# Packing three column groups into one expert unit of a mixture-of-experts layer: 46 units in place of 52

## What is computed

```python
gates = jnp.einsum('tk,tke->te', wsel, jax.nn.one_hot(eidx, N_EXPERTS, dtype=wsel.dtype))
def expert(acc, xs):
    wg, wu, wd, ge = xs
    y = (jax.nn.silu(x @ wg) * (x @ wu)) @ wd
    return acc + ge[:, None] * y.astype(jnp.float32), None
routed, _ = lax.scan(expert, jnp.zeros((n_tok, shp[-1]), jnp.float32), (w_gate, w_up, w_down, gates.T))
```

## Time and profile before

| | us |
|---|---|
| median of 3 runs | 1839.17 |
| lowest and highest | 1833.34, 1845.14 |
| the profiled execution | 1832.0 |
| its span, first to last instruction | 1830.3 |

### The profile page before, as it was taken

The page is one execution under the profiler, slowest core; times in us unless marked ns, Lnnn a source line. Parts: engine busy times, 40 slices in busy tenths (PEclk is TensorE's granted clock), DMA queues, the critical chain, the costliest instruction groups (busy, mean ns, idle before and its releaser), DMA issues. The chain is left out here.

```text
span 1830.3 us, 19726 instructions
## 1 busy us (share of the span) xinstructions
PE 1645.5 (90%) x7369; PEld 952.7 (52%) x7369; DVE 669.5 (37%) x1267; ACT 340.6 (19%) x680; POOL 323.3 (18%) x338
## 2 busy tenths in 40 slices
PE   5998888999858979999687987999999999999966
PEld 3856665664347767877473443344444444444423
DVE  2001333343378493442454973241111111111128
ACT  1001233423222121222110220011111111111120
POOL 5000000000039990000000251011111111111100
PEclk8996899999988999999798999999999999999989
DMA  9213010113131214230924004999999999989756
GB/s 342 81 46 101 24 47 1 47 47 109 56 96 52 99 62 116 83 114 9 336 88 155 35 21 187 388 418 421 407 418 399 401 379 400 407 352 421 283 199 256
DMA packets 114556, 361.54 MB, mean 198 GB/s; under 512 B 37803, under 2 KB 37931, under 8 KB 88339
## 3 DMA queue, kind: packets, MB, share of 16 engines
q1 hardware_dynamic: 89734, 308.53, 43.7%
q0 software_dynamic: 16112, 35.89, 5.1%
q10 hardware_dynamic: 8614, 15.84, 2.5%
HBM read 336.07 MB, written 43.01 MB: 207 GB/s over the span
## 5 line engine op out<-in xcount | busy, mean ns | idle before, releaser
L1835 PE MATMUL bank<-arena 128*64 128x512 f32 (+1 forms) x1152 | 369.7, 600 | 2.7 <-DMA arena<-in_w_up 2.7
L1835 PEld LDWEIGHTS bank<-arena 128*64 128x64 f32 (+1 forms) x1152 | 139.9, 162 | 195.2 <-issue 195.2
L1843 PE MATMUL bank<-arena 128*64 128x512 f32 (+1 forms) x576 | 190.3, 599 | 0.9 <-DVE arena L2539 0.9
L1183 PE MATMUL bank<-arena 128*128 128x272 f32 x512 | 129.4, 403 | 20.2 <-PEq L1045 19.2
L2533 DVE TENSOR_TENSOR arena<-arena,bank 128x256 f32<-128x256 f32 x52 | 21.9, 421 | 335.2 <-ACT arena L2213 335.2
L1822 POOL DMA_INDIRECT expert_rows<-arena x52 | 52.4, 1007 | 500.0 <-PE bank L1828 445.5
L424 PE MATMUL bank<-arena 128*128 128x512 f32 (+4 forms) x384 | 126.5, 490 | 10.5 <-DVE arena L2342 8.1
L416 PE MATMUL bank<-arena 128*128 128x272 f32 x512 | 123.4, 405 | 12.2 <-DVE arena L1711 6.2
L1843 PEld LDWEIGHTS bank<-arena 128*64 128x64 f32 (+1 forms) x576 | 68.1, 160 | 117.9 <-issue 116.8
L416 PEld LDWEIGHTS bank<-arena 128*128 128x128 f32 x512 | 100.7, 197 | 34.3 <-DVE arena L1711 6.6
L1183 PEld LDWEIGHTS bank<-arena 128*128 128x128 f32 x512 | 95.4, 193 | 44.5 <-issue 21.8
(11 more groups left out here) (423 smaller groups left out, 2117.8 us busy)
## 6 DMA issues: line engine op xcount, KB each, us to landing
arena<-in_w_gate SPq DMA_DIRECT2D x64, 1024.0 KB, 12.2
arena<-in_w_up SPq DMA_DIRECT2D x64, 1024.0 KB, 18.5
arena<-in_w_down SPq DMA_DIRECT2D x64, 1024.0 KB, 17.5
arena<-in_w_ada SPq DMA_DIRECT2D x12, 2048.0 KB, 9.6
arena<-in_w_in SPq DMA_DIRECT2D x11, 2048.0 KB, 9.0
arena<-expert_rows SPq DMA_DIRECT2D x8, 2048.0 KB, 25.2
gate_logits<-arena ACTq DMA_DIRECT2D x16, 272.0 KB, 3.0
arena<-gate_logits SPq DMA_DIRECT2D x8, 544.0 KB, 5.6
```

Of the source, the lines that this page charges most:

```text
L1183: mm = nc.tensor.matmul(out[:, 0:HALF], w[:, k, m * P:(m + 1) * P], hT[:, k, half * HALF:(half + 1) * HALF], start=k == 0, stop=k == KD - 1)
L1835: mm = nc.tensor.matmul(out[rows].rearrange("p (a n) -> p a n", a=2), x[:, k, rows], gate_up_slot(n)[:, :, k, :], start=k == 0, stop=k == ...
L1843: mm = nc.tensor.matmul(out[rows, :], h[:, k, rows], down_slot(n)[:, k, 512 * half:512 * half + 512], start=k == 0, stop=k == 1)
```

## The change

The 20 units of two experts and the 32 of one become 14 of two, 20 of one and 12 of a new kind T:

- ranks 20 to 31, which had a whole unit each, take rows 0 to 95 of a unit (cap 96 in place of 128);
- ranks 52 to 63, which had 64 rows each in N units, take rows 96 to 127 (cap 32 in place of 64);
- the 96 rows are cut into a column group of 64 and one of 32, so each k step of a T unit is three products with 64, 32 and 32 stationary columns, at partitions 0, 64 and 96.

The number of weight loads stays 64, the rows gathered and scattered stay the same, and the order in which the units of a block follow each other is new.

```diff
-HEAVY, WIDE, PAIRED = 8, 32, 40
+HEAVY, THREE, WIDE, PAIRED, SMALL = 8, 20, 32, 40, 52
+def segments(*loads_rows):
+
+    at_, out = 0, []
+    for load, rows in loads_rows:
+        while rows:
+            n = P if rows == P else 64 if rows >= 64 else QUAD
+            out.append((slice(at_, at_ + n), load))
+            at_, rows = at_ + n, rows - n
+    return out
+
+
+pairs = iter(range(6))
 for blk in range(4):
-    wide, paired = iter(range(6)), iter(range(3))
-    for kind in "XPWNWWNXPWNWW":
+    heavy, wide, three = iter(range(2)), iter(range(3)), iter(range(3))
+    for kind in ("XPTWNWTXPTWN", "XPTWTWNXPTW")[blk % 2]:
...
+        elif kind == "T":
+            i = 4 * next(three) + blk
+            LOADS += [THREE + i, SMALL + i]
+            UNITS.append((THREE + i, segments((n, 96), (n + 1, QUAD))))
...
-            for rows, cap in ((E, 64.0), (WIDE, 128.0), (HEAVY, 192.0)):
+            for rows, cap in ((E, 32.0), (SMALL, 64.0), (WIDE, 96.0), (THREE, 128.0), (HEAVY, 192.0)):
...
-                unit_mm.inc(nc.tensor.transpose(bank[5][:, 2 * E:3 * E], ranked[:, P:2 * P], ident[0:E, 0:E]))
+                nc.tensor.transpose(bank[5][:, 2 * E:3 * E], ranked[:, P:2 * P], ident[0:E, 0:E])
+                unit_mm.inc(nc.tensor.transpose(bank[5][:, 3 * E:4 * E], quad.rearrange("p a n -> p (a n)"), ident[0:E, 0:E]))
...
             def gate_up_of(u):
-                parts = parts_of(UNITS[u][1])
+                parts = UNITS[u][1]
...
+                step(nc.vector.tensor_copy(quad, ranked[:, 0:QUAD].unsqueeze(1).to_broadcast([E, 4, QUAD])))
                 done(dup_done, nc.vector.tensor_copy(twice, ranked[:, 0:64].unsqueeze(1).to_broadcast([E, 2, 64])))
...
+                step(nc.vector.tensor_copy(units_f[last, THREE:WIDE], got[last, 3 * E + SMALL:4 * E]))
```

More of the change, by code:

```diff
@@ L51 @@
 UNITS, LOADS = [], []
+def segments(*loads_rows):
[7 more added lines that the diff above has]
+pairs = iter(range(6))
 for blk in range(4):
-    wide, paired = iter(range(6)), iter(range(3))
-    for kind in "XPWNWWNXPWNWW":
+    heavy, wide, three = iter(range(2)), iter(range(3)), iter(range(3))
+    for kind in ("XPTWNWTXPTWN", "XPTWTWNXPTW")[blk % 2]:
         n = len(LOADS)
         if kind == "X":
-            r = blk if n == 16 * blk else 4 + blk
+            r = 4 * next(heavy) + blk
             LOADS.append(r)
-            UNITS.append((r, (n,)))
+            UNITS.append((r, segments((n, P))))
         elif kind == "P":
             LOADS.append(WIDE + r)
-            UNITS.append((WIDE + r, (n - 1, n)))
+            UNITS.append((WIDE + r, segments((n - 1, 64), (n, 64))))
         elif kind == "W":
             LOADS.append(HEAVY + 4 * next(wide) + blk)
-            UNITS.append((LOADS[-1], (n,)))
-        else:
-            i = 4 * next(paired) + blk
-            LOADS += [PAIRED + i, PAIRED + 12 + i]
-            UNITS.append((PAIRED + i, (n, n + 1)))
+            UNITS.append((LOADS[-1], segments((n, P))))
+        elif kind == "T":
+            i = 4 * next(three) + blk
+            LOADS += [THREE + i, SMALL + i]
+            UNITS.append((THREE + i, segments((n, 96), (n + 1, QUAD))))
+        else:
+            i = next(pairs)
+            LOADS += [PAIRED + i, PAIRED + 6 + i]
+            UNITS.append((PAIRED + i, segments((n, 64), (n + 1, 64))))
 NU = len(UNITS)
-LAST_UNIT = {load: u for u, (_, loads) in enumerate(UNITS) for load in loads}
+LAST_UNIT = {load: u for u, (_, parts) in enumerate(UNITS) for _, load in parts}
 class Tick:
@@ L1765, in build @@
     ranked = at(X0 + 12800, LC, p=E)
-    twice = at(X0 + 13568, 2, 64, p=E)
+    twice, quad = at(X0 + 13568, 2, 64, p=E), at(X0 + 13696, 4, QUAD, p=E)
     units_f, floor_f = at(T2, NU), at(T2 + NU, NU)
@@ L1844, in down_half @@
         return mm
-    def parts_of(loads):
-        return [(slice(0, P), loads[0])] if len(loads) == 1 else [(slice(0, 64), loads[0]), (slice(64, P), loads[1])]
     one = [(slice(0, P), 0)]
@@ L2483, in unit_indices @@
                 got = bank[5]
-                low, high = slice(0, 64), slice(64, P)
+                low, high, last = slice(0, 64), slice(64, P), slice(96, P)
                 step(nc.vector.tensor_copy(units_f[:, 0:WIDE], got[:, 0:WIDE]))
+                step(nc.vector.tensor_copy(units_f[last, THREE:WIDE], got[last, 3 * E + SMALL:4 * E]))
                 step(nc.vector.tensor_copy(units_f[low, WIDE:PAIRED], got[low, 2 * E:2 * E + HEAVY]))
                 step(nc.vector.tensor_copy(units_f[high, WIDE:PAIRED], got[high, E + WIDE:E + PAIRED]))
-                step(nc.vector.tensor_copy(units_f[low, PAIRED:NU], got[low, E + PAIRED:E + PAIRED + 12]))
-                step(nc.vector.tensor_copy(units_f[high, PAIRED:NU], got[high, E + PAIRED + 12:2 * E]))
+                step(nc.vector.tensor_copy(units_f[low, PAIRED:NU], got[low, E + PAIRED:E + PAIRED + 6]))
+                step(nc.vector.tensor_copy(units_f[high, PAIRED:NU], got[high, E + PAIRED + 6:E + SMALL]))
                 done(unit_done, row_indices(step, units_f, floor_f, to_rows, from_rows))
```

## The result

| | before | after |
|---|---|---|
| median of the runs, us | 1836.45 (4 runs, 1833.34 to 1845.14) | 1923.09 (4 runs, 1906.37 to 1929.32) |
| profiled span, us | 1830.3 | 1920.0 |
| mean granted TensorE clock | 0.942 | 0.945 |

The ratio is 1.0461, with a 95% interval of 1.0425 to 1.0498: the kernel is slower by 87 us, against 1928 us forecast. Six units fewer, and more time on TensorE.

What follows compares the result with a forecast made beforehand. TensorE was taken as the bound, DMA nearly as full. Terms 303.6 - 209.5 - 5.7 + 0.3 = +88.7 us on a median of 1839.2 gave 1928 us, range 1908 to 1948, or 1890 to 1975 with the second rival and partial overlap.

Steps and rivals of the forecast that it cites:

- TensorE sets the pace, and unequal products do not share the array.: Expert stage: TensorE waits 3.6 us in 600; products of 64 and 32 columns run serially, not side by side.
- The doubt it named: On the evidence from L699 and L700 (64, then 8 contracted rows, no overlap): same bank, and row tiles, not column tiles.
- the telling rows: Trace rows of L699 and L700, on disjoint partitions: L700 starts 1.05 us behind L699, read as no overlap.
- A k step of 1.98 us: T unit's three products: 1.00 us for 64 columns plus 0.98 for two of 32; a single has 0.86; range 1.88 to 2.10.
- A T unit of 25.3 us: TensorE's price for one T unit, 11.41 - 10.3 + 23.8 + 0.4; twelve are 303.6 us.
- -5.7 us at the fourth unit: Fourth unit's 2.70 us wait for weights goes, as do its slower products (10.04 us in place of 7.09).
- +0.3 us for the table of rows: One more 64x128 copy on DVE and one more transpose on TensorE delay TensorE's next product by 0.3 us.
- The sum: Whole kernel: 303.6 - 209.5 - 5.7 + 0.3 = +88.7 us, on a median of 1839.2, forecast 1928 us.
- 303.6 - 209.5 - 5.7: Expert stage: twelve T units added, 12 single units and 6 units of two removed, fourth unit's wait and slow products gone.
- the 2.24 at which the array would empty at every pass: T units: four size changes per k step make it 2.24 us, twelve T units 37 us dearer, 1965 us; chance 0.08.
- the third rival: T units: clock falls as only half the columns work at a time, +286 us, 2210 us; chance 0.02.
- The first rival: T units: 64, 32 and 32 share the array at 12.1 us a unit, DMA becomes the bound, 1792 us; chance 0.13.

## Why the prediction was right, step by step

- **TensorE sets the pace, and unequal products do not share the array.** Right, and shown in the column direction, which no row of the kernel before could do. The doubt it named (the telling rows were row tiles that add into one bank) is settled for columns by two pairs of runs in which nothing but the cut differs, all groups in one bank: in the changed kernel 64, 32 and 32 take 15.88 us and four of 32 take 7.01; in the kernel before 15.88 and 7.00. What kept L699 and L700 apart, their sizes or their common bank, no run tells. The page TensorEngine Tiling (Array Packing) of the Trainium skill, section Tiling Modes, states that a change of tiling mode drains TensorE. The traces agree as far as they go: the loads of the other size come only 0.98 to 1.00 us later, and a change cost 0.14 us.
- **A k step of 1.98 us.** Measured 1.99 (1383.44 to 1385.43); gate and up 15.88 against 15.9. The range around it was reckoned a little narrow: from 1.98 down to 1.88 twelve T units move by 14 us, up to 2.10 by 17 and not 14.
- **A T unit of 25.3 us.** Measured 25.2.
- **-5.7 us at the fourth unit.** Its wait is gone from the list of waits, as said, and its gate and up, from 1186.20 on, last 7.03 us and not 10.
- **+0.3 us for the table of rows.** It can't be told. The first unit's gate and up starts at 1144.5 us after and at 1141.3 us before, but in runs whose code ahead of the stage is that of before it starts at 1143, 1148 and 1151 us; the start of the stage wanders by more than this term.
- **The sum.** Forecast +88.7; the spans differ by 89.7, the medians by 86.6. Of the 4.8 us between 1928 and 1923, 2.7 come from the median of before, which was taken as 1839.17 and is 1836.45 with a fourth run. That the spans came within 1 us is in part luck. From the first gate and up to the end of the last down products the stage grew by 86.9 us (1141.34 to 1754.92 before, 1144.51 to 1844.98 after), against 303.6 - 209.5 - 5.7 = 88.4 reckoned; the later start of the stage brought the other 3.2.
- **The other rivals.** A k step of 1.99 us is far from the 2.24 at which the array would empty at every pass. The granted clock was 1.00 in every stretch of the stage from 1194 us on, although half of the columns stood empty in the T units, so the third rival is out.
- **The first rival's price was too low.** That the three groups share the array was given 0.13, at 1792 us. The version that has the sharing, by four equal groups, takes 1808.68. Its products end 24 us earlier than before (the last down starts at 1727.20 and lasts 3.70 us), where 47 were reckoned, and two terms make the difference. The smaller is DMA's pace: the sum used 421 GB/s for the whole stage. In the stretch from 1131 to 1711 us of that version the view of DMA gives a mean of 408:

```profile
GB/s 361 416 346 409 412 421 423 418 421 420 423 422 420 414 421 421 422 418 416 405 414 422 403 403 414 424 420 421 383 411 418 422 420 410 417 422 424 419 414 193
DMA packets 40836, 236.39 MB, mean 408 GB/s; under 512 B 7401, under 2 KB 7401, under 8 KB 16609
```

236.39 MB at 408 is 579 us, where 421 would give 561; the stretch starts ten us ahead of the rival's 1141. The last slice is less than half full, so by an estimate from it the weights are in near 1704, 6 us later than the 1698 reckoned. The larger term is what follows: some 27 us of products and not 10, which is 17 us. The end of the stage does not hang on the last weights: TensorE's last wait for weights ends at 1667.57, and from there it works through the last five units without another, 63 us to the end at 1730.90.

## What to carry to other kernels

In these runs (float32 products that stream 512 columns) column groups of TensorE worked side by side only while they were of one size: pack 96 and 32 rows as four groups of 32, never as 64, 32 and 32, and cut all parts of a step to the size of the smallest. Four products of 32 columns cost what two of 64 did, and a change of size cost some 0.14 us, so keep the sizes apart in time where they must be mixed. And before packing more work into TensorE's time, look at the second bound: here six units fewer were worth 61 us with some of the weights left out, and 25 with all of them, where DMA at 408 GB/s is right behind.

## What had not been expected of the hardware

- A TensorE that counts as busy 100% of a stretch can have half its columns idle: the changed kernel's stage and that of before read alike in busy time and in granted clock (1.00), at 25.2 and 12.1 us a unit.
- The changes between sizes are cheap against what they prevent: of the 13 us that a T unit costs over a unit of two, some 3 are changes.
- Where TensorE waited for weights 10 times for 30 us, the granted clock of the stretches fell to 0.96 to 0.98. In the version with four equal groups the longest wait is this one:

```profile
1198.09 9.74 PE L1853 MATMUL bank<-arena 128*64 128x512 f32 x32 [7.32 <-DMA arena<-in_w_up]
```

The gate and up behind it took 9.7 us in place of 7.0, with a mean granted clock of 0.73 from 1198 to 1208 us, so the lower level for about half of them. Gate and up behind six of the ten waits lasted 1.7 to 2.7 us longer than elsewhere, 12.9 us together. Behind the other four, of 1.10, 1.15, 1.76 and 3.04 us, they kept their length, while behind one of 2.02 us they did not. In all, 30 us of waits for weights came with 12.9 us of slower products, and the length of a wait alone did not say whether any would follow.
